# Layer embedding on four pairs of banks, forget logits behind the last key, merge's first gate in three pieces, weight splits moved up at six places

## The reference

```python
x = x + 0.5 * swiglu(rms_norm(x, ffn1_norm), ...)            # ffn1, width 2816
h = rms_norm(x, mix_norm)
y_fox = forgetting_attention(rms_norm(fq), rms_norm(fk), fv, log_sigmoid(f_logit + forget_bias))
y_sb = stick_breaking_attention(sq, sk, sv)
x = x + (sigmoid(g_fox) * (y_fox @ w_fox) + sigmoid(g_sb) * (y_sb @ w_sb)) @ w_out
x = x + 0.5 * swiglu(rms_norm(x, ffn2_norm), ...)            # ffn2
x = x + sigmoid(rms_norm(x, ple_norm) @ w_ple_gate) * (p @ w_ple_proj)   # layer embedding
# second block: a Hyena branch (long convolutions by filter spectra) and latent attention (mla), merged
```

## Time and profile before

| what | value |
|---|---|
| median of 3 runs | 1810.55 us (1810.22 to 1813.80) |
| profiled execution | 1812.15 us, span 1810.3 us |
| PE busy | 1758.9 us, 97% of the span |
| mean granted clock of PE | 0.992 |

### The profile page before, as it was taken

One profiled execution on the slowest core, in us unless ns is written; L12 is line 12 of the kernel. 1 busy time (PEld: TensorE's weight loads), 2 busy tenths in 40 slices (PEclk: granted clock), 3 DMA queues, 4 the chain that ended last, 5 costly groups with the idle time before them and its releaser, 6 DMA issues.

```text
span 1810.3 us, 21484 instructions
## 1 busy us (share of the span) xinstructions
PE 1758.9 (97%) x7776; PEld 1413.5 (78%) x7776; DVE 1068.7 (59%) x1173; ACT 633.3 (35%) x883; POOL 743.5 (41%) x319
## 2 busy tenths in 40 slices
PE   7999999999999999999999999999999999898999
PEld 6887888877787887887887788878776667787887
DVE  6777367765553465476764466777426642959541
ACT  5222222225544755222222222222445643332321
POOL 2443344433322421444444344434363433747443
PEclk9999999999999999999999999999999999999999
DMA  4332232324211210333332223322420123222243
GB/s 178 97 105 92 81 105 93 112 81 175 70 59 59 94 58 24 113 120 96 116 109 96 93 93 101 104 87 94 168 76 23 31 95 127 70 93 91 91 132 117
DMA packets 45232, 172.89 MB, mean 95 GB/s; under 512 B 5177, under 2 KB 5177, under 8 KB 44380
## 3 DMA queue, kind: packets, MB, share of 16 engines
q1 hardware_dynamic: 39888, 150.75, 25.7%
q10 hardware_dynamic: 5260, 20.94, 3.2%
HBM read 161.05 MB, written 10.62 MB: 95 GB/s over the span
## 4 chain that ended last, share of the span: by engine, by line
issue 59%; PE 21%; POOL 17%; DVE 1%; ACT 1%; POOLq 1%; DMA 0%; SPq 0%; DVEq 0%; ACTq 0%
POOL wlo L259 16%; PE psum L293 6%; PE psum L295 6%; PE psum L294 6%; PE psum L1573 2%; POOL scratch L2421 1%; PE psum L1562 1%; PE psum L1534 0%; POOLq L267 0%; ACT whi L281 0%; DMA xT<-x_dram 0%; ACT mprob L1721 0%; PE psum L1528 0%; DVE small L1842 0%; POOLq L257 0%
## 5 line engine op out<-in xcount | busy, mean ns | idle before, releaser
L259 POOL TENSOR_TENSOR wlo<-raw,whi 128x1024 fp32r<-128x1024 f32 (+3 forms) x266 | 674.3, 2536 | 991.8 <-ACT whi L281 991.7
L293 PE MATMUL psum<-h_hi,whi 128*128 128x512 f32 x1360 | 540.9, 398 | 12.8 <-POOL wlo L259 10.8
L281 ACT ACTIVATE whi<-raw 128x1024 fp32r<-128x1024 f32 (+3 forms) x267 | 291.9, 1094 | 742.9 <-PE psum L295 738.6
L295 PE MATMUL psum<-h_hi,wlo 128*128 128x512 f32 x1360 | 531.5, 391 | 0.0
L294 PE MATMUL psum<-h_lo,whi 128*128 128x512 f32 x1360 | 531.3, 391 | 0.0
L293 PEld LDWEIGHTS psum<-h_hi,whi 128*128 128x128 f32 x1360 | 256.7, 189 | 73.7 <-POOL wlo L259 14.5
L294 PEld LDWEIGHTS psum<-h_lo,whi 128*128 128x128 f32 x1360 | 256.9, 189 | 55.1 <-issue 3.1
L295 PEld LDWEIGHTS psum<-h_hi,wlo 128*128 128x128 f32 x1360 | 256.5, 189 | 54.7
L293 PE MATMUL psum<-mid_hi,whi 128*128 128x512 f32 x352 | 138.1, 392 | 0.0
L294 PE MATMUL psum<-mid_lo,whi 128*128 128x512 f32 x352 | 137.0, 389 | 0.0
L295 PE MATMUL psum<-mid_hi,wlo 128*128 128x512 f32 x352 | 137.0, 389 | 0.0
(11 more groups left out here) (335 smaller groups left out, 2504.2 us busy)
## 6 DMA issues: line engine op xcount, KB each, us to landing
raw<-wk_dram SPq DMA_DIRECT2D x220, 512.0 KB, 3.7
raw<-wd_dram SPq DMA_DIRECT2D x32, 704.0 KB, 4.1
raw<-wp_dram SPq DMA_DIRECT2D x8, 640.0 KB, 3.9
spectra_scratch<-spec_out ACTq DMA_DIRECT2D x8, 512.0 KB, 6.5
x_scratch<-xT ACTq DMA_DIRECT2D x2, 2048.0 KB, 9.1
xT<-x_scratch ACTq DMA_DIRECT2D x8, 512.0 KB, 4.3
spec<-spectra_scratch ACTq DMA_DIRECT2D x2, 2048.0 KB, 10.2
raw<-wq_dram SPq DMA_DIRECT2D x8, 320.0 KB, 2.9
```

Source lines behind the costliest of these rows:

```text
L259: pool.tensor_tensor(wlo[s][:, 0:w], raw[s][:, 0:w], whi[s][:, 0:w].bitcast(F32), ALU.subtract).then_inc(lo_ready, 1)
L281: act.activation(whi[s][:, 0:w], raw[s][:, 0:w], ACT.Copy).then_inc(hi_ready, 1)
L293: pe.matmul(dst, s_hi, m_hi, start=start and i == 0, stop=False, **kw)
L295: last = pe.matmul(dst, s_lo, m_hi, start=False, stop=stop and i == n - 1, **kw)
```

## The change

Six parts:

1. In both feed-forward blocks ACT splits the sixth unit between the sigmoids of tiles 0 and 1, not behind both.
2. In front of both norms (mix and block2) the table of Ln and Exp is loaded ahead of the wait for the first spectra unit; the third spectra unit is split ahead of the norm's factor, the next unit after four of the eight tiles, and the one after it behind the eighth. At the latent attention one more split stands ahead of a Square and three DMA issues.
3. The split of the forget logits and their copies (8 in all) come behind the eighth tile, on ACT behind two more splits.
4. The first gate unit of the merge runs in pieces of three, two and three: the last three stand between the last two `tensor_outputs`.
5. p is split at the start of ffn2's second half.
6. In the layer embedding tile b has banks 2(b mod 4) and the one above it. The product and x's summand stay in PSUM, the square is taken by ACT into the gate's bank, and DVE adds it up. The loops are written out. PE waits for a bank's squares from the fifth tile on, where it waited for x of the tile before last.

```diff
-            def factor(self, act):
-
-                act.preload_act_table_set("natural_log_exp_and_others")
+            def factor(self, act, table=True):
+
+                if table:
+                    act.preload_act_table_set("natural_log_exp_and_others")
                 act.wait_ge(self.mean, self.i + 1)
                 act.activation(std[:, :], bank(7), ACT.Ln, scale=1.0 / (self.n * P),
                                bias=col("eps")).then_inc(self.std, 1)
...
             def scalar(self, act, splits=None):
-                self.factor(act)
+                self.factor(act, False)
...
                         self.norm.factor(act)
                         act.preload_act_table(ACT.Sigmoid)
                         sigmoid(0)
+                        split_hi_to(act, up + 6)
                         sigmoid(1)
-                        split_hi_to(act, up + 6)
                         filters.load(act, self.order)
                     else:
                         split_hi_to(act, up + 2)
                         filters.scalar_unit(act, self.order, 0)
+                        if self.order:
+                            ple.scalar_inputs(act)
                         split_hi_to(act, up + 3)
                         sigmoid(0)
                         filters.store_unit(act, self.order, 0)
...
                         filters.vector_unit(dve, self.order, 0)
+                        if self.order:
+                            ple.vector_inputs(dve)
                     hidden_tile(0, 0, 0 if half else 2)
                     if half == 0:
                         hidden_tile(1, 0, 4)
...
                             self.scalar_softplus(act)
-                        if i == 6:
-                            act.wait_ge(self.forget, 7)
-                            act.wait_ge(filters.stored, 64)
-                            for h in range(1, HEADS, 2):
-                                act.activation(fk_lo[other[1], h, :], forgets[other[1], :],
-                                               ACT.Copy).then_inc(self.softplus, 1)
                 split_hi_to(act, BASE["fox_v"] + 4)
+                act.wait_ge(self.forget, 7)
+                act.wait_ge(filters.stored, 64)
+                for h in range(1, HEADS, 2):
+                    act.activation(fk_lo[other[1], h, :], forgets[other[1], :], ACT.Copy).then_inc(self.softplus, 1)
                 split_hi_to(act, BASE["fox_v"] + 5)
                 act.wait_ge(unit_done, BASE["fox_v"] + 4)
                 for t, b in ((1, 6), (2, 4), (3, 5)):
...
                         self.vector_steps(dve)
                     elif i == 4:
                         self.vector_sums(dve)
-                    elif i == 5:
-                        self.vector_split_sums(dve)
-                    elif i == 6:
-                        for h in range(0, HEADS, 2):
-                            dve.tensor_copy(fk_lo[other[0], h, :],
-                                            forgets[other[0], :].bitcast(F32)).then_inc(self.forget, 1)
+                self.vector_split_sums(dve)
+                for h in range(0, HEADS, 2):
+                    dve.tensor_copy(fk_lo[other[0], h, :], forgets[other[0], :].bitcast(F32)).then_inc(self.forget, 1)
                 dve.wait_ge(unit_done, BASE["fox_v"] + 4)
                 dve.tensor_copy(v32[:, 0, :], bank(7)).then_inc(merge1.seven_read, 1)

...
                         merge1.tensor_part(pe, h + 2, 7)
+                    elif h == 6:
+                        merge1.tensor_first_gate(pe, 0, 3)
                     else:
-                        merge1.tensor_first_gate(pe, DT // 2 * (h - 6))
+                        merge1.tensor_first_gate(pe, 3, 2)
                     self.tensor_sums(pe, h)
                     self.tensor_outputs(pe, h - 1)
+                merge1.tensor_first_gate(pe, 5, 3)
                 self.tensor_outputs(pe, HEADS - 1)
...
+            def banks(self, b):
+                return bank(2 * (b % 4)), bank(2 * (b % 4) + 1)
...
+                for b in range(DT):
+                    gate_bank, add_bank = self.banks(b)
+                    pe.wait_ge(lo_ready, self.base + b + 1)
+                    if b == 1:
+                        pe.wait_ge(x_updated, self.x_base)
+                    elif b == 3:
+                        pe.wait_ge(self.norm.std, self.norm.i + 1)
+                    elif b >= 4:
+                        pe.wait_ge(summed, SUMS["block2"] - DT + b - 3)
+                    linear(pe, gate_bank, self.base + b, h_hi, h_lo, DT, signal=False,
+                           chunk_ready=self.norm.ready if b == 0 else None, ready_base=self.norm.base)
+                    if b == 0:
                         pe.wait_ge(self.p_ready, 1)
...
+                    linear(pe, add_bank, self.base + b, p_hi, p_lo, 2, first=DT)
+                    if b == 0:
+                        self.norm.tensor(pe)
...
-            def scalar(self, act):
+            def scalar_inputs(self, act):
                 act.wait_ge(self.landed, 16)
                 act.activation(p_hi[:, :, :], p32[:, :, :], ACT.Copy).then_inc(self.hi, 1)
...
+            def vector_inputs(self, dve):
                 dve.wait_ge(self.hi, 1)
                 dve.tensor_tensor(p_lo[:, :, :], p32[:, :, :], p_hi[:, :, :].bitcast(F32),
                                   ALU.subtract).then_inc(self.p_ready, 1)
...
+            def scalar(self, act):
+                self.norm.factor(act)
+                act.preload_act_table(ACT.Sigmoid)
+                for b in range(DT):
+                    split_hi_to(act, self.base + b + 3)
+                    act.wait_ge(self.gate, b + 1)
+                    act.activation(ple_gate[b % 2][:, :], ple_gate[b % 2][:, :], ACT.Sigmoid).then_inc(self.sig, 1)
+                    act.wait_ge(x_updated, self.x_base + b + 1)
+                    act.activation(self.banks(b)[0], xT[:, b, :], ACT.Square).then_inc(self.square, 1)
...
+                for b in range(DT):
+                    gate_bank, add_bank = self.banks(b)
+                    dve.wait_ge(unit_done, self.base + b + 1)
+                    dve.tensor_tensor(ple_gate[b % 2][:, :], gate_bank, rstd[:, :], ALU.mult).then_inc(self.gate, 1)
+                    dve.wait_ge(self.sig, b + 1)
+                    dve.tensor_tensor(add_bank, ple_gate[b % 2][:, :], add_bank, ALU.mult).then_inc(self.add, 1)
+                    dve.wait_ge(self.add, b + 1)
+                    dve.tensor_tensor(xT[:, b, :], xT[:, b, :], add_bank, ALU.add).then_inc(x_updated, 1)
+                    counts["x"] += 1
+                    self.vector_sum(dve, b)
+
+            def vector_sum(self, dve, b):
+                dve.wait_ge(self.square, b + 1)
+                dve.wait_ge(summed, counts["sum"])
+                dve.tensor_tensor(sumsq[:, :], sumsq[:, :], self.banks(b)[0], ALU.add).then_inc(summed, 1)
+                counts["sum"] += 1
...
                 split_hi_to(act, u + 2)
+                act.wait_ge(unit_done, u + 1)
+                split_hi_to(act, u + 3)
                 self.scalar_square(act, 0)
...
                 pe.wait_ge(lo_ready, u + 1)
+                if o and m:
+                    pe.wait_ge(*((ple.square, 8) if m == 2 else (summed, SUMS["block2"] - 1)))
                 if m == 2:
...
             split_hi_to(act, BASE["spectra0_rest"] + 2)
+            act.preload_act_table_set("natural_log_exp_and_others")
             filters.scalar_unit(act, 0, 1)
-            norm_mix.scalar(act, {0: BASE["fox_q"], 4: BASE["fox_q"] + 1})
+            split_hi_to(act, BASE["fox_q"])
+            norm_mix.scalar(act, {3: BASE["fox_q"] + 1})
+            split_hi_to(act, BASE["fox_q"] + 2)
             filters.scalar_unit(act, 0, 2)
             filters.scalar_unit(act, 0, 3)
...
             mla.load(act)
+            act.preload_act_table_set("natural_log_exp_and_others")
             filters.scalar_unit(act, 1, 1)
-            norm_block2.scalar(act, {0: BASE["mla_cq"], 4: BASE["mla_cq"] + 1})
+            split_hi_to(act, BASE["mla_cq"])
+            norm_block2.scalar(act, {3: BASE["mla_cq"] + 1})
+            split_hi_to(act, BASE["mla_cq"] + 2)
             filters.scalar_unit(act, 1, 2)
             filters.scalar_unit(act, 1, 3)
```

More of the change, by code:

```diff
@@ L1333, in vector_part, with tensor_first_gate @@
                 dve.tensor_tensor(xT[:, b, :], xT[:, b, :], bank(at_bank), ALU.mult).then_inc(self.part, 1)
-            def tensor_first_gate(self, pe, first):
+            def tensor_first_gate(self, pe, first, n):
                 if first == 0:
@@ L1338, in tensor_first_gate @@
                     pe.wait_ge(self.part, DT)
-                linear_piece(pe, bank(7), self.base, h_hi, h_lo, first, DT // 2, DT)
+                linear_piece(pe, bank(7), self.base, h_hi, h_lo, first, n, DT)
             def wait_gate_banks(self, pe, p):
@@ L1363, in __init__ @@
                 self.norm, self.x_base, self.base = norm, x_base, BASE["ple"]
```

(25 more changed lines are left out.)

31 lines of the change are left out of this document (1 added, 30 removed).

## The result

The changed kernel takes 1793.32 us (median of 4 runs, 1793.13 to 1793.34), the kernel before 1811.68 us beside it (4 runs, 1810.22 to 1813.80): a ratio of 0.9897, 95% interval 0.9880 to 0.9914. The profiled executions have spans of 1791.3 and 1810.3 us, 19.0 apart. The forecast was taken off the median of 1810.55 us that stood on record ahead of it.

A forecast was written before the change was run, and what follows sets the result against it. PE, busy 1758.9 us, was taken as the bound, with its idle waits and low clock to be won. Gains of 16.4 us off the 1810.55 us median gave 1794.2 us, own range 1791.5 to 1796.5, with rivals 1789 to 1801.

The forecast's parts named there:

- second feed-forward block: PE's 2.51 us stall at 859.60 becomes 0.6, for the seventh unit's `wlo`: gain 1.9 us.
- low clock: Half-clock stretches behind PE's stalls at 473.56 and 859.60 go, 1.7 us each: 3.4 us.
- first feed-forward block: PE's 2.51 us stall at 41.14 becomes 1.7, as DVE is held beside POOL's earlier subtraction: gain 0.8 us.
- mixing norm: The 1.86 us stall for `wlo` goes, 0.4 comes at the second query unit: gain 1.4 us.
- forget attention: The 4.09 us wait for ACT's Ln goes, 0.5 comes at the third value unit: gain 3.6 us.
- merge's first gate: PE's 1.49 us wait for DVE's split L1157 becomes 0.2 at the last sums: gain 1.3 us.
- layer embedding, second norm: Waits for p, x, the norm's sum and the next `wlo` go, but for 0.2: gain 4.0 us.
- The forecast's own sign of being wrong: In PE's timeline after the change, low-clock stretches standing where there were none would show the forecast wrong.
- the sign for the second block: In the second feed-forward block, a `wlo` wait of 0.3 to 0.9 us with clock 1.00 would show it right.
- Rival 1: DVE isn't held beside POOL and nothing is late next: 20.2 us gained, 1790.3 us; chance 0.17.
- Rival 2: Feed-forward stalls only move on, low clock returns behind shorter waits: 10.3 or 12 us gained, 1798.5 to 1800.3; chance 0.25.

The follow-up runs named there:

- e8: The changed kernel with the splits and the table load around the mixing norm put back as before: 1794.47 us (one run).
- e2: The changed kernel with the forget logits' split and their eight copies back among the eight tiles: 1801.08 us.
- e10: The changed kernel with the first gate unit of the merge in two pieces of four again: 1795.96 us (one run).
- e3: The changed kernel with the layer embedding of before and p split at its start, the second norm's splits kept: 1798.76 us.
- e7: The changed kernel run once more, unchanged: 1794.56 us.
- e5_gate_first: The changed kernel with filter loads issued before the second sigmoid and DVE scaling the next gate ahead of the tile's split, in both feed-forward blocks: 1789.64 us.
- e9: The changed kernel with silu times up kept in its PSUM bank and read there by the split, filter loads left in place: 1790.37 us.

## Why the prediction was right

1794.2 us was forecast and 1793.32 measured. The mechanism held in the main; of the terms of the sum, two had the wrong size. The second feed-forward block gave 1.5 less than its term, and the other five 1.15 more, so that the idle terms, 13.0 in all, met 12.7. The low clock gave 6.6 where I had 3.4. In idle time, with the clock in the last line:

| term | forecast | measured | by |
|---|---|---|---|
| first feed-forward block | 0.8 | 1.03 | 2.51 to 1.48 |
| second feed-forward block | 1.9 | 0.44 | 2.51 to 2.07 |
| mixing norm | 1.4 | 1.86 | e8: 1.87 |
| forget attention | 3.6 | 3.76 | e2: 4.09 to 0.33 |
| merge's first gate | 1.3 | 1.49 | e10: 1.49 |
| layer embedding, second norm | 4.0 | 4.11 |: 1.50, 0.88, 1.09, 0.86 to 0.22; 3.1 of it by e3 |
| low clock | 3.4 | 6.6 | busy, 1758.9 to 1752.3 |

- **First feed-forward block**: each step as written. L610 held until 37.9 where I had 37.1 to 37.3, in a program that had started 0.8 us later; a second gate late; a stall of 1.48 where I had 1.7.
- **Second feed-forward block**: the step that failed is "`wlo` is ready at 863.1 ... a stall of 0.6". The `wlo` was 0.47 late, but I had followed only the stream of weights. The same hold that I charged to the first subtraction also met the second one, and PE waits for DVE's third gate too and gets it late: 2.07 us of wait where I had 0.6. I had asked what is late next on ACT and POOL, and not on DVE.
- **Mixing norm, merge**: the rests of 0.4 and 0.2 that I put down for what is late next were too careful. PE found the second query unit ready, and the last sums too.
- **Forget attention**: 0.33 left where I had 0.5, for the `wlo` of the third value unit, as forecast. Why the 3.48 of L964 and the 2.19 of the copies could both be moved for nothing shows in the idle sum: nothing else waits.
- **Layer embedding**: no bracket for p, x or the norm's sum, 0.22 for the third unit's `wlo` where I had 0.2. The chain takes 4.67 us where I had 5.3, since ACT's split (1.27) isn't part of it: the six operations add up to 4.0, and 0.7 are handoffs.
- **Low clock**: "the low stretch behind the 4.09 goes: 1.7" and the same at 859.60 took the stretches for properties of their stalls. The 6.6 has two halves in this pair of profiles: the two stretches that I named, and about as much from the last fifth of the program, of which the forecast said nothing. e7 showed that each wait of over 2 us draws them or not from one execution to the next. What can be said of the change is that it leaves seven waits of over 2 us where there were nine, and that busy fell by 6.6 in this pair of profiles. Two executions of the changed kernel differed by up to 5.6 us, two of the kernel before by 12.2; beside e7 the medians are 1794.56 and 1810.25, 15.7 apart (ratio 0.9918, 0.9898 to 0.9938) where the first comparison has 18.4. The 16.4 of the forecast lies between them, and that it met the first median to 0.9 us is partly luck. The forecast's own sign of being wrong, low stretches where there were none, is met by e7 at 1617 and 1648; the sign for the second block (0.3 to 0.9, clock 1.00) was missed too. Why one wait draws a stretch and the next doesn't stays open. The Trainium skill says ("TensorE: Matmul & The Clock Gate", Part 1) that what gates the clock runs free of the kernel's start, which would fit. The runs agree so far that the fall keeps no fixed distance to its wait. These are windows around the end of the same wait of 2.15 us, at 1332.07 in e5_gate_first and at 1342.14 in e3_no_emb:

```profile
1331.50:1332.00 0.50, 0.00 (x0) 0.94 0.00 0
1332.00:1332.50 0.50, 0.43 (x1) 0.50 0.91 128
```

```profile
1342.00:1343.20 1.20, 1.06 (x5) 1.00 0.68 151
1343.30:1344.00 0.70, 0.70 (x5) 0.50 0.39 150
```

In the first the clock falls before the wait ends, in the second over 1 us behind it, with five matmuls begun in between. Whether the same shift decides that it falls at all is not shown.

Rival 1 (DVE isn't held, 1790.3) fell with L612's 2.22. e9 shows what that case would have given in idle time, 30.93; that its median of 1790.37 meets the rival's 1790.3 says little, with single executions from 1786.03 to 1791.44. Rival 2 had the right event (a stall behind the stall, in the second block) but not its size, 2.07 of 2.51. Its other half, low clock coming back behind a shorter wait, did happen in e7, behind the 2.07, though not in the first profile.

## What to carry to other kernels

Where a wait is removed by moving work earlier on one engine, look up what else runs at the new time, on all engines: here the subtraction that moved ahead of a gate held DVE's operations on SBUF, and what was won came back partly as a wait for DVE. Giving the held operations a PSUM operand, or putting those that somebody waits for ahead of those that can be held, took it away, at a price that PE didn't feel (0.26 us more of DVE for the copy). And judge an edit by the waits of the profile, which behind the first matmul repeat to 0.1 us, before the times, which here moved by 5.6 us and, for the kernel before, by 12.2.

## What the runs showed of the hardware

- Beside a POOL subtraction DVE's split is held or not by where its input lies: a copy with one SBUF input and an SBUF output took 2.22 us (0.43 alone), one with a PSUM input 0.69; subtractions with two SBUF inputs 2.76, with one in PSUM 0.69. The single input of the copy, which the prediction counted in favour of its first rival, didn't free it.
- The low clock (0.50, 1.2 of 2.4 GHz) came, but for the end of the program, only in waits of 2.06 us and more or up to 1.5 us behind them, in pieces that cost 1.7 us or 3.4 us, and not behind the same wait in each execution of the same program. Of the changed kernel's seven such waits, three had it in one profile and five in the other, and only one (near 1512) in both.
- The start isn't the same either. PE's wait near 45 began at 46.33 − 1.48 = 44.85 in the changed kernel and at 44.56 − 1.47 = 43.09 in e2_no_fox, with the same instructions before it. The matmuls began 0.43 us apart until 14.25 in the one and until 10.62 in the other, and 0.23 apart from there on. That is about the pace of the stretches at 0.50 (13 matmuls in 5.68 us), but the record has 1.00 for both: a granted clock of 1.00 in the first microseconds doesn't show full pace.
